# Five places for split output weights in the last pair, splits three ahead, mixed rows behind them

## The chip, the cores and the metric

The kernel runs on one NeuronCore of one Trainium2 chip. The metric is the device time of one execution in microseconds (us). PE is the matmul engine (TensorE), DVE is VectorE, ACT is ScalarE, POOL is GpSimd, and SP (SyncE) issues most of the DMAs. Each engine works through its own queue in order and is held to the others by semaphores alone, which are all written by hand in this kernel.

## The reference

One layer of a hybrid decoder trunk over 1024 tokens of width 2048, in fp32:

```
h = rms_norm(x, norm_g)
aq, ak, av, az, bq, bk, bv, bz, bf, cq, ck, cv, cz, cr = split(h @ w_in)
out_a = dilated_mixture(rms(aq), rms(ak), av)          # 12 heads, three dilated windows mixed
out_b = forgetting_attention(rms(bq), rms(bk), bv, cumsum(log_sigmoid(bf + bias)))   # 8 heads
out_c = rms(gla_chunked(cq, ck, cv, log_a))            # 4 heads, gated linear attention
mixed = concat(out_a * silu(az), out_b * silu(bz), out_c * silu(cz))
out   = x + mixed @ w_out
```

## The kernel before

**Split numbers.** Each fp32 product is made of three matmuls in a rounded format: an operand is split into a high part (ACT copies it into fp32r) and a low part (DVE subtracts), and PE does hi*hi, hi*lo and lo*hi. So a tile of weights must be loaded (SP), split by ACT, split by DVE, and then PE can use it. Such a weight tile is 128 x 512.

**Stages.** First x is normalised and transposed into `act_hi` and `act_lo` (16 rows k of 128 x 1024 each). Then projection groups run one after another: each has 16 k-steps in four quarters, and other work is woven between the quarters in eight slots a group. The work woven in is first that of the four GLA heads, then of ten attention pairs (two heads each; six of A, four of B). The last pair (`LAST` = 9) has only one projection group left (`S_LAST_Z`, slots 0 to 7). From slot 8 to 32 the output projection of the first 512 columns is woven in instead: 45 quarters called "early 0" to "early 44" here (`early_quarter`), in three rounds of 15. A round covers three, three and two token tiles (`ROUNDS`), since three PSUM banks are free, and goes through 15 of the 16 rows of the mixed activations. A quarter n of a round takes row k = `OUT_ORDER[n % 15]`. After the last pair come the first column group's remaining row (k=9), and the other column groups over all eight tiles (`out_quarter`).

**The mixed rows.** In slots 4 to 13 of the last pair the gated outputs of the heads are read back from DRAM over `act_lo`'s rows (`load_mixed`, two rows at a time) and split in place: ACT writes `act_hi`'s row, DVE `act_lo`'s (`mix_hi_part`, `mix_lo_part`, in the slot that `MIX_SLOT` gives). Row k=8 is that of the pair before and is taken from the tile `vz`. z of the last pair is loaded into `vz` only when this has been done, and its gate follows in slots 15 to 18.

**Places.** Raw output weights have four places (`EARLY_RAWS`), split ones three (`EARLY_SPLITS`): `w_hi`/`w_lo` have two, `extra_hi`/`extra_lo` one. ACT and DVE do the split of n+2 in the slot of early n. Their order inside a slot is: the pair's own steps with the mixed rows at their end, a split, the late steps of the slot, and the other splits.

**The pair's own steps** are written out by `steps_of`. An item j is one block of 128 queries of a head: scores on PE (L2038, L2040 for the causal part, L2041), bias and maximum on DVE (L1661), exponential on ACT (L1226), scaling on DVE (L1669, L1671). A unit u gathers such blocks: PE turns them (L2049), ACT and DVE split the result (L1234, L1677), and PE multiplies with the values (L2064). The steps that the prediction speaks of, by slot (a bar marks the late half; the early quarters stand where they are issued):

```
slot  8: product 1, scale 4, score 5, finish 1, early 0 | early 1
slot  9: scale 5, early 2 | early 3
slot 10: turn 2, early 4 | early 5
slot 11: product 2, turn 3, early 6 | score 6, early 7
slot 12: early 8 | product 3, scale 6, score 7
slot 13: early 9 | scale 7, early 10
slot 14: early 11 | turn 4, early 12
slot 15: early 13 | product 4, turn 5, early 14
slot 16: score 8, score 9, gate of the last pair, early 15 | early 16
slot 17: product 5, scale 8, scale 9, early 17
slot 18: turn 6, early 18 | early 19
slot 28: early 36 | scale 15, early 37
slot 29: early 38 | turn 10, early 39
```

**Early lines.** The early matmuls are L2113 to L2115, their splits L972 (ACT) and L1776 (DVE); a mixed row is L1334 (ACT) and L1797 (DVE); raw weights are loaded by L671, z by L471, the residual tiles by L716; sums of partials are L1791. The first column group's own splits are L958 and L1783, its matmuls L2154 to L2156.

**In a GLA head**, level l takes differences on DVE (L1519, L1520), exponentials on ACT (L1109), products on POOL (L881, L883) and eight matmuls on PE (L1945). DVE's masked copies into `weights_t` (L1568) follow each level; `put_first` does four of them for level 0 in one slot.

Of the kernel before, what the change touches and what calls it, by code (L numbers as in the profile page):

```python
# [15 lines left out]
P = 128  # L16
# [3 lines left out]
NT = SEQ // P  # L20
# [88 lines left out]

ROUNDS = ((0, 1, 2), (3, 4, 5), (6, 7))  # L110
EARLY = len(ROUNDS) * (KT - 1)
EARLY_RAWS, EARLY_SPLITS = 4, 3
EARLY_SLOT = [8 + (n * 5) // 9 for n in range(EARLY)]
MIX_SLOT = [4, 4, 5, 6, 6, 7, 8, 9, 9, 10, 10, 11, 12, 12, 13]

OUT_ORDER = list(range(LAST - 1)) + [LAST + 1, LAST + 2, LAST - 1] + list(range(LAST + 3, KT)) + [LAST]
KK_GATED = OUT_ORDER.index(LAST - 1)
MIX_LOADS = [k for k in range(0, KT, 2) if k != LAST - 1]
MIX_BUFS = 4
# [57 lines left out]
def score_offset(j):  # L177

    i = j % NT
    return HALF * (i % 2) if i < 4 else 0  # L180


def head_columns(c):
# [44 lines left out]
def build(nc, x, norm_g, w_in, a_q_gain, a_k_gain, b_q_gain, b_k_gain, fox_bias,  # L228
# [11 lines left out]
    with ExitStack() as ctx:  # L240
# [135 lines left out]
        last.close()  # L376

        early_raws = [extra_raw[:, 0, :], w_raw[:, 0, :], extra_raw[:, 1, :], w_raw[:, 1, :]]
        early_his = [w_hi[:, 0, :], extra_hi[:], w_hi[:, 1, :]]
        early_los = [w_lo[:, 0, :], extra_lo[:], w_lo[:, 1, :]]  # L380

        def mix_row(k):

# [76 lines left out]
        def _(sp):  # L460
# [278 lines left out]
            load_mixed(3)  # L739
            load_early_rows(2)  # L740
            load_early_rows(3)
            load_mixed(4)
            load_mixed(5)
            load_mixed(6)
            for n in range(4, EARLY):
                load_early_rows(n)
                if n == 6:
                    sp.wait_ge(mix_lo, KK_GATED + 1)
                    load_gate(LAST, last_column)
                if n == 7:  # L750

                    sp.wait_ge(silu_done, LAST)
                    for t in range(4):
                        load_early_residual(t)
                for r, tiles in enumerate(ROUNDS[:-1]):
                    if n == (KT - 1) * (r + 1) + 3:
                        for t in tiles:
                            store_partial(t)
                        for t in ROUNDS[r + 1]:
                            if t >= 4:  # L760
                                load_early_residual(t)
# [163 lines left out]
        def _(act):  # L925
# [20 lines left out]
            def split_hi_out(cg, kk):  # L946

                slot = kk % 2
                if kk == 1:

                    if isinstance(cg, int) and cg == 1:
                        act.wait_ge(partial_ready, NT)
                    else:
                        act.wait_ge(out_ready, NT * (cg - 1))
                else:
                    act.wait_ge(quarter_done, 3 * (GROUPS + AHEAD) + EARLY - len(ROUNDS) + (KT - 1) * (cg - 1) + kk - 1 + (kk == 0))
                act.wait_ge(w_in_sem[slot], 16 * (2 * (GROUPS + AHEAD) + EARLY // 4 + (KT // 2) * (cg - 1) + kk // 2 + 1))
                act.activation(w_hi[:, slot, :], w_raw[:, slot, :], ACT.Copy).then_inc(hi_done, 1)  # L958
# [332 lines left out]
            def last_body():  # L1291
                def steps(slot):
                    steps_at(LAST, 2 * slot, False)
                    for kk in range(KT - 1):
                        if MIX_SLOT[kk] == slot:
                            mix_hi_part(kk)

                def late(slot):
                    steps_at(LAST, 2 * slot + 1, False)

                def split_last(s, kq):
                    if kq < 4:
                        split_hi(s, kq)
                    else:
                        split_hi_early(0)

                group(S_LAST_Z, COL_B + 3 * B_WIDTH + (B_PAIRS - 1) * P, steps, split_after=split_last,
                      late=late)
                split_hi_early(1)
                for slot in range(8, SLOTS + 1):  # L1310
                    steps(slot)
                    for n in early_at(slot)[:1]:
                        split_next(n + 2)
                    late(slot)
                    for n in early_at(slot)[1:]:
                        split_next(n + 2)

            def split_next(n):
                if n < EARLY:
                    split_hi_early(n)  # L1320
                elif n == EARLY:
                    split_hi_out(1, 0)

            def mix_hi_part(kk):
                k = OUT_ORDER[kk]
                if k == LAST - 1:
                    act.wait_ge(o_done, LAST)
                    act.wait_ge(quarter_done, 3 * (S_LAST_Z + AHEAD) + k // 4 + 1)
                elif k == LAST:
                    act.wait_ge(o_done, LAST + 3)  # L1330
                else:
                    i = MIX_LOADS.index(k // 2 * 2)
                    act.wait_ge(mix_in[i % MIX_BUFS], 16 * (i // MIX_BUFS + 1))
                act.activation(act_hi[:, k, :], mix_row(k), ACT.Copy).then_inc(mix_hi, 1)  # L1334
# [20 lines left out]
        def _(dve):  # L1355
# [134 lines left out]
            def gla_steps(c, slot):  # L1490
# [19 lines left out]
                for l in range(LEVELS):  # L1510
                    if slot == G_LEVEL[l]:
# [6 lines left out]
                        dve.wait_ge(gla_ql, n - 1 if l >= 2 else LEVELS * c)  # L1518
                        dve.tensor_tensor(ev[:, :, 1, :], bv[:, :, 1, :], edge, ALU.subtract).then_inc(gla_diff, 1)  # L1519
                        dve.tensor_tensor(ev[:, :, 0, :], edge, bv[:, :, 0, :], ALU.subtract).then_inc(gla_diff, 1)  # L1520
                if slot == G_LEVEL[0] + 2:
                    put_first(c)
                for l in range(1, LEVELS - 1):
                    if slot == G_LEVEL[l] + 2:
                        put_level(c, l)
# [41 lines left out]
                dve.reg_add(levels_put, levels_put, 1)  # L1567
                dve.copy_predicated(dst, mask.bitcast(I32), data).then_inc(gla_put, 1)  # L1568

            def put_first(c):  # L1570
                dve.wait_ge(gla_zero, c + 1)
                dve.wait_ge(gla_lv, LEVELS * c + 1)
                for half in range(2):
                    to = weights_t[:, half * HALF:(half + 1) * HALF].rearrange("p (b u q) -> p b u q", b=2, u=2)
                    if half > 0:
                        dve.wait_ge(gla_put, levels_put)
                    put(to, ident_both[:, :, :].unsqueeze(1).broadcast_to([P, 2, 2, P]), pieces[half][:, :, :, 0:P])
                    dve.wait_ge(gla_put, levels_put)
                    put(to.rearrange("p b u (n two) -> p b u n two", two=2)[:, :, :, :, 1],
                        level_mask[:, 0, :, :].unsqueeze(1).broadcast_to([P, 2, 2, HEAD]),  # L1580
                        pieces[half][:, :, :, P:])

            def put_level(c, l):
                b = 1 << l
# [153 lines left out]
            def last_body():  # L1738
                def steps(slot):
                    steps_at(LAST, 1, 2 * slot, None)  # L1740
                    for kk in range(KT - 1):
# [12 lines left out]
                group(S_LAST_Z, steps, split_after=split_last, late=late)  # L1754
                split_lo_early(1)
                for slot in range(8, SLOTS + 1):
                    for n in early_at(slot):
                        if n % (KT - 1) == 0 and n > 0:
                            early_sums(n // (KT - 1) - 1)
                    steps(slot)  # L1760
                    for n in early_at(slot)[:1]:
                        split_next(n + 2)
                    late(slot)
                    for n in early_at(slot)[1:]:
                        split_next(n + 2)

            def split_next(n):
                if n < EARLY:
# [62 lines left out]
        def _(pe):  # L1831
# [191 lines left out]
            def score(pair, j, kind):  # L2023
                h, i = j // NT, j % NT
                n = (i + 1) * P
                if i == 0:
                    pe.wait_ge(ql_done, 2 * pair + h + 1)
                    pe.wait_ge(kl_done, 2 * pair + h + 1)
                    pe.wait_ge(k_other_done, 2 * pair + h + 1)

                if first_pair(pair) and i == 0:
                    pe.wait_ge(k_zeroed, h + 1)
                o = score_offset(j)
                pe.wait_ge(masked, ITEMS * pair + j - (o > 0))
                q = q_st[:, h, i * P:(i + 1) * P]
                for c0 in range(0, n, HALF):
                    c1 = min(c0 + HALF, n)
                    pe.matmul(scores[:, o + c0:o + c1], q, k_hi[:, h, c0:c1], start=True, stop=False)  # L2038
                    if kind == 1 and c1 == n:
                        pe.matmul(scores[:, o + i * P:o + n], ident_r[:], causal_r[:], start=False, stop=False)  # L2040
                    mm = pe.matmul(scores[:, o + c0:o + c1], q, k_lo[:, h, c0:c1], start=False, stop=True)  # L2041
                mm.then_inc(s_done, 1)
# [148 lines left out]
```

## Time and profile before

| | |
|---|---|
| median of 3 runs | 2104.77 us (2103.35 to 2106.62) |
| the profiled execution | 2104.9 us, span 2103.2 us |
| mean granted PE clock | 0.993 |
| busy PE / DVE / ACT / POOL | 2050.0 / 970.3 / 858.4 / 249.5 us |
| last pair from early 0 to the first column group | 1699.4 to 1831.7 us of the span |

Times in the trace are from the start of the span. A row of the timeline gives start, duration, engine, line, operation, tiles and shape, and in brackets how long the engine sat idle before it and what ended that. Matmuls are pipelined: the time that one takes is the distance to the start of the next, and its duration is modelled.

### The profile page before, as it was taken

To read this page: it belongs to the slowest core of one execution; us is meant where nothing else is said; L and a number is where in the kernel's file an instruction comes from. 1 tells how busy PE (TensorE), PEld (TensorE's weight loads), DVE (VectorE), ACT (ScalarE), POOL (GpSimd) and SP (SyncE) were. 2 spreads that over 40 slices of the span, in tenths; PEclk is the share of its full clock that TensorE was granted. 3 is DMA by queue.
4 is the path that set the end of the run, shared out by engine and by line. 5 is a ranking of instruction groups with operands and counts; after the bars stand their busy time and mean duration, and the time that the engine had idled before them with its cause. 6 is when DMAs were issued, how large, how long until landed. Compare 5 with 4: busy or idle time off the path is not lost.

```text
span 2103.2 us, 28249 instructions
## 1 busy us (share of the span) xinstructions
PE 2050.0 (97%) x10120; PEld 1717.1 (82%) x10120; DVE 970.3 (46%) x1579; ACT 858.4 (41%) x1434; POOL 249.5 (12%) x181
## 2 busy tenths in 40 slices
PE   6999999999999999999999999999999988999999
PEld 5778888888878888888888888888888867788887
DVE  6611356455544544554454544554544465512122
ACT  6311344434444444454544444454544454311110
POOL 0000344252420101010010101010010100000000
PEclk9999999999999999999999999999999999999999
DMA  6322323433232222222222222223222363324134
GB/s 224 78 75 65 108 76 104 108 89 108 69 101 76 71 88 58 86 74 89 61 70 85 75 86 86 81 81 100 60 90 85 129 210 113 125 89 130 47 128 150
DMA packets 192457, 201.09 MB, mean 96 GB/s; under 512 B 15993, under 2 KB 141993, under 8 KB 191233
## 3 DMA queue, kind: packets, MB, share of 16 engines
q1 hardware_dynamic: 175664, 169.70, 27.2%
q10 hardware_dynamic: 16720, 30.45, 3.9%
q8 instruction: 43, 0.70, 0.1%
q14 instruction: 30, 0.24, 0.0%
HBM read 151.33 MB, written 48.78 MB: 95 GB/s over the span
## 4 chain that ended last, share of the span: by engine, by line
PE 84%; DVE 7%; ACT 4%; issue 3%; DMA 2%; POOL 1%; SPq 0%; DVEq 0%; ACTq 0%; POOLq 0%
PE acc L1851 18%; PE acc L1853 18%; PE acc L1852 18%; PE pv L2064 4%; PE turned L2049 4%; PE scores L2041 2%; PE scores L2038 2%; DVE w_lo L1360 1%; PE scores L2154 1%; PE scores L2155 1%; PE turned L2155 1%; PE acc L2155 1%; PE scores L2156 1%; PE turned L2156 1%; PE acc L2156 1%
## 5 line engine op out<-in xcount | busy, mean ns | idle before, releaser
L1851 PE MATMUL acc<-act_hi,w_hi 128*128 128x512 f32 x1856 | 743.0, 400 | 7.5 <-DVE act_lo L1391 2.4
L1853 PE MATMUL acc<-act_hi,w_lo 128*128 128x512 f32 x1856 | 725.8, 391 | 0.0
L1852 PE MATMUL acc<-act_lo,w_hi 128*128 128x512 f32 x1856 | 724.2, 390 | 0.0
L1851 PEld LDWEIGHTS acc<-act_hi,w_hi 128*128 128x128 f32 x1856 | 349.4, 188 | 77.1 <-DVE w_lo L1360 5.0
L1853 PEld LDWEIGHTS acc<-act_hi,w_lo 128*128 128x128 f32 x1856 | 348.6, 188 | 76.1
L1852 PEld LDWEIGHTS acc<-act_lo,w_hi 128*128 128x128 f32 x1856 | 349.7, 188 | 65.1
L1360 DVE TENSOR_TENSOR w_lo<-w_raw,w_hi 128x512 fp32r<-128x512 f32 x223 | 196.2, 880 | 317.4 <-ACT w_hi L934 317.4
L1677 DVE TENSOR_TENSOR pt_lo<-turned,pt_hi 128x1024 fp32r<-128x1024 f32 (+1 forms) x120 | 114.9, 958 | 256.0 <-ACT pt_hi L1234 255.0
L1226 ACT ACTIVATE prob<-prob,neg_max 128x128 f32<-128x128 f32 (+7 forms) x160 | 124.1, 776 | 251.5 <-DVE neg_max L1661 251.5
L1234 ACT ACTIVATE pt_hi<-turned 128x1024 fp32r<-128x1024 f32 (+1 forms) x120 | 97.6, 813 | 244.7 <-PE turned L2049 244.7
L934 ACT ACTIVATE w_hi<-w_raw 128x512 fp32r<-128x512 f32 x223 | 139.0, 623 | 128.8 <-PE acc L1853 105.4
L908 POOL TENSOR_TENSOR q_st<-raw,q_st 64x1024 fp32r<-64x1024 f32 x20 | 49.4, 2472 | 994.1 <-ACT q_st L1203 994.1
L1661 DVE CUSTOM_DVE_ANT_0 prob<-scores,logit_bias 128x128 f32<-128x128 f32 (+7 forms) x160 | 118.2, 753 | 40.1 <-PE scores L2041 38.4
L1783 DVE TENSOR_TENSOR w_lo<-w_raw,w_hi 128x512 fp32r<-128x512 f32 x49 | 33.9, 693 | 213.9 <-ACT w_hi L958 213.9
L958 ACT ACTIVATE w_hi<-w_raw 128x512 fp32r<-128x512 f32 x49 | 31.0, 632 | 229.6 <-PE side L2156 209.8
L978 ACT ACTIVATE stage<-acc 128x512 f32<-128x512 f32 x112 | 66.7, 595 | 112.8 <-PE acc L1853 112.8
L2049 PE MATMUL turned<-ident,prob 128*128 128x128 f32 x720 | 100.2, 276 | 0.4 <-DVE prob L1671 0.3
L2049 PEld LDWEIGHTS turned<-ident,prob 128*128 128x128 f32 x720 | 85.2, 142 | 13.2 <-DVE prob L1671 2.4
L2064 PE MATMUL pv<-pt_lo,v_st 128*128 128x256 f32 (+1 forms) x400 | 94.2, 290 | 0.0
L2064 PE MATMUL pv<-pt_hi,v_st 128*128 128x256 f32 (+1 forms) x400 | 87.6, 269 | 0.3 <-DVE pt_lo L1677 0.3
L2038 PE MATMUL scores<-k_hi,q_st 128*128 128x512 f32 (+1 forms) x240 | 82.8, 347 | 3.9 <-DVE neg_max L1661 2.7
L1671 DVE TENSOR_SCALAR prob<-prob,inv_denom 128x128 f32<-128x128 f32 (+7 forms) x160 | 83.3, 521 | 5.7
(308 smaller groups left out, 2723.2 us busy)
## 6 DMA issues: line engine op xcount, KB each, us to landing
w_raw<-in_w_in_dram SPq DMA_DIRECT2D x240, 256.0 KB, 2.8
proj_scratch<-stage ACTq DMA_DIRECT2D x116, 256.0 KB, 2.1
w_raw<-in_w_out_dram SPq DMA_DIRECT2D x71, 256.0 KB, 3.0
raw<-proj_scratch SPq DMA_DIRECT2D x20, 512.0 KB, 3.2
act_lo<-mixed_scratch SPq DMA_DIRECT2D x7, 1024.0 KB, 6.7
res<-in_x_dram SPq DMA_DIRECT2D x24, 256.0 KB, 5.5
out_dram<-res SPq DMA_DIRECT2D x24, 256.0 KB, 2.8
extra_raw<-in_w_out_dram SPq DMA_DIRECT2D x23, 256.0 KB, 3.2
```

Source lines behind the costliest of these rows:

```text
L934: act.activation(w_hi[:, slot, :], w_raw[:, slot, :], ACT.Copy).then_inc(hi_done, 1)
L1226: act.activation(prob[:, j % 2, 0:n], prob[:, j % 2, 0:n], ACT.Exp, scale=-1.0, bias=neg_max[:, j:j + 1], accum_out=denom[:, j:j + 1]).the ...
L1234: act.activation(pt_hi[:, 0:n], turned[:, 0:n], ACT.Copy).then_inc(pth_done, 1)
L1360: dve.tensor_tensor(w_lo[:, slot, :], w_raw[:, slot, :], w_hi[:, slot, :].bitcast(F32), ALU.subtract)\
L1661: dve.tensor_tensor_reduce(out=prob[:, j % 2, 0:n], in0=scores[:, c0:c0 + n], in1=bias, scale=1.0, scalar=3e38, op0=ALU.add, op1=ALU.min, ...
L1677: dve.tensor_tensor(pt_lo[:, 0:n], turned[:, 0:n], pt_hi[:, 0:n].bitcast(F32), ALU.subtract)\
L1851: pe.matmul(acc, hi, xh, start=first, stop=False)
L1852: pe.matmul(acc, hi, xl, start=False, stop=False)
L1853: mm = pe.matmul(acc, lo, xh, start=False, stop=end)
L2038: pe.matmul(scores[:, o + c0:o + c1], q, k_hi[:, h, c0:c1], start=True, stop=False)
L2049: mm = pe.transpose(turned[:, o:o + P], prob[:, q, c * P:(c + 1) * P], ident[:])
L2064: mm = pe.matmul(pv[:, (2 * (d % 2) + q) * P:(2 * (d % 2) + 2) * P], v_st[:, h, c, :], (pt_hi, pt_lo)[part][:, o:o + (2 - q) * P], start=( ...
```

## The change

Four edits are made together.

1. **Output weights in the last pair.** Split weights have five places. The two new ones are halves of row k=9 (`LAST`) of `act_hi` and `act_lo`, which is not read from the last projection quarter that needs it until its own mixed row is written. ACT and DVE do the split of n+3 in the slot of early n. Mixed rows from slot 8 on are split at the end of their slot, behind the splits; the last three stand in slots 13, 14 and 14 and not in 12, 12 and 13. Row k=8 now comes ninth in the order of rows (it was the eleventh). SP loads the later mixed rows between the loads of raw weights, z of the last pair and four residual tiles behind raw weight 10 (before: behind 6 and 7), and stores partials two loads later.
2. **Waits that follow from it.** The first two splits of the first column group wait for the last quarter that used their place, and the mixed row of k=9 waits for all eight partials.
3. **Scores of item 4** (and 12) of every pair stand at column offset 128 of their two banks and not at 0, so that their 640 columns are done as 384 and 256 and not as 512 and 128.
4. **GLA**: the four masked copies of `put_first` are done in two slots, two in each.

```diff
-EARLY_RAWS, EARLY_SPLITS = 4, 3
+EARLY_RAWS, EARLY_SPLITS, EARLY_AHEAD = 4, 5, 3
-MIX_SLOT = [4, 4, 5, 6, 6, 7, 8, 9, 9, 10, 10, 11, 12, 12, 13]
-OUT_ORDER = list(range(LAST - 1)) + [LAST + 1, LAST + 2, LAST - 1] + list(range(LAST + 3, KT)) + [LAST]
+MIX_SLOT = [4, 4, 5, 6, 6, 7, 8, 9, 9, 10, 10, 11, 13, 14, 14]
+OUT_ORDER = list(range(LAST)) + list(range(LAST + 1, KT)) + [LAST]
...
-    return HALF * (i % 2) if i < 4 else 0
+    return HALF * (i % 2) if i < 4 else P * (i == 4)
...
-        early_his = [w_hi[:, 0, :], extra_hi[:], w_hi[:, 1, :]]
-        early_los = [w_lo[:, 0, :], extra_lo[:], w_lo[:, 1, :]]
+        early_his, early_los = ([w[:, 0, :], more, w[:, 1, :], row[:, LAST, 0:HALF], row[:, LAST, HALF:]]
+                                for w, more, row in ((w_hi, extra_hi[:], act_hi), (w_lo, extra_lo[:], act_lo)))
...
-            load_mixed(4)
-            load_mixed(5)
-            load_mixed(6)
             for n in range(4, EARLY):
+                if n < 7:
+                    load_mixed(n)
                 load_early_rows(n)
-                if n == 6:
+                if n == 10:
                     sp.wait_ge(mix_lo, KK_GATED + 1)
                     load_gate(LAST, last_column)
-                if n == 7:
+                if n == 10:
                     sp.wait_ge(silu_done, LAST)
                     for t in range(4):
                         load_early_residual(t)
                 for r, tiles in enumerate(ROUNDS[:-1]):
-                    if n == (KT - 1) * (r + 1) + 3:
+                    if n == (KT - 1) * (r + 1) + 5:
...
-                if kk == 1:
-                    if isinstance(cg, int) and cg == 1:
-                        act.wait_ge(partial_ready, NT)
-                    else:
-                        act.wait_ge(out_ready, NT * (cg - 1))
+                if isinstance(cg, int) and cg == 1 and kk < 2:
+                    user = (EARLY - 1 - 2 * kk) // EARLY_SPLITS * EARLY_SPLITS + 2 * kk
+                    act.wait_ge(quarter_done, 3 * (GROUPS + AHEAD) + user + 2 - len(ROUNDS))
+                elif kk == 1:
+                    act.wait_ge(out_ready, NT * (cg - 1))
...
-                split_hi_early(1)
+                for n in range(1, EARLY_AHEAD):
+                    split_hi_early(n)
                 for slot in range(8, SLOTS + 1):
                     steps(slot)
                     for n in early_at(slot)[:1]:
-                        split_next(n + 2)
+                        split_next(n + EARLY_AHEAD)
                     late(slot)
                     for n in early_at(slot)[1:]:
-                        split_next(n + 2)
+                        split_next(n + EARLY_AHEAD)
+                    mixed_of(slot)
...
                 elif k == LAST:
+                    act.wait_ge(partial_ready, NT)
                     act.wait_ge(o_done, LAST + 3)
...
-                if slot == G_LEVEL[0] + 2:
-                    put_first(c)
+                for half in range(2):
+                    if slot == G_LEVEL[0] + 2 + half:
+                        put_first(c, half)
...
-                for c0 in range(0, n, HALF):
-                    c1 = min(c0 + HALF, n)
+                edge = min(HALF - o % HALF, n)
+                for c0, c1 in ((0, edge), (edge, n))[:1 + (edge < n)]:
```

`last_body` is changed in the same way on DVE, with `mix_lo_part` and `split_lo_early`.

## Rows read from the trace of the kernel before

**Rows 1.** The page: busy time, share of the span and instructions of each engine.
```profile
PE 2050.0 (97%) x10120; PEld 1717.1 (82%) x10120; DVE 970.3 (46%) x1579; ACT 858.4 (41%) x1434; POOL 249.5 (12%) x181
```

**Rows 2.** Table by stretches: PE, PEld, DVE, ACT, POOL busy; granted clock; DMA.
```profile
1699.40:1755.90 56.50, 45.30 (x192) 36.03 (x193) 31.95 (x45) 24.75 (x36) 0.00 (x0) 0.88 0.39 133
...
1699.40:1831.70 132.30, 115.18 (x533) 93.27 (x533) 75.56 (x125) 57.40 (x94) 0.00 (x0) 0.94 0.40 132
```

**Rows 3.** PE's waits, 1690 to 1840: us in total, times, longest us.
```profile
PE acc L2113 <- DVE w_lo L1776: 11.5, 6, 3.7
PE acc L2113 <- DVE extra_lo L1776: 3.8, 2, 3.6
...
PE scores L2154 <- DVE w_lo L1783: 0.7, 1, 0.7
```

**Rows 4.** Timeline, ACT and PE before early 2: start, us, what, [idle before].
```profile
1704.07 1.04 ACT L1334 ACTIVATE act_hi<-act_lo 128x1024 fp32r<-128x1024 f32 x1
1705.02 0.62 ACT L972 ACTIVATE w_hi<-extra_raw 128x512 fp32r<-128x512 f32 x1
...
1707.03 0.79 PE L2113 MATMUL acc<-w_hi,act_hi 128*128 128x512 f32 x1 [3.23 <-DVE w_lo L1776]
```

**Rows 5.** Timeline, SP, ACT and PE around the weights of early 7.
```profile
1718.90 0.43 SPq L671 DMA_DIRECT2D w_raw<-in_w_out_dram  x1
...
1724.61 0.63 ACT L972 ACTIVATE extra_hi<-w_raw 128x512 fp32r<-128x512 f32 x1 [7.22 <-DMA w_raw<-in_w_out_dram]
...
1726.02 0.50 PE L2113 MATMUL acc<-extra_hi,act_hi 128*128 128x512 f32 x1 [3.60 <-DVE extra_lo L1776]
```

**Rows 6.** Timeline, PE: item 8's score; start of early 21; the turn after early 24.
```profile
1755.86 0.22 PE L2038 MATMUL scores<-k_hi,q_st 128*128 128x128 f32 x1
...
1774.32 0.39 PE L2113 MATMUL acc<-w_hi,act_hi 128*128 128x512 f32 x1
...
1782.59 0.93 PE L2049 MATMUL turned<-ident,prob 128*128 128x128 f32 x7
```

**Rows 7.** Timeline: DVE at unit 2's turn; ACT and PE before early 11.
```profile
1715.01 1.23 DVE L1677 TENSOR_TENSOR pt_lo<-turned,pt_hi 128x1024 fp32r<-128x1024 f32 x1 [2.72 <-ACT pt_hi L1234]
...
1740.20 0.61 ACT L972 ACTIVATE w_hi<-w_raw 128x512 fp32r<-128x512 f32 x1
...
1742.21 0.79 PE L2113 MATMUL acc<-w_hi,act_hi 128*128 128x512 f32 x1 [3.67 <-DVE w_lo L1776]
```

**Rows 8.** Timeline, PE and DVE around early 17 and unit 6's turn.
```profile
1764.13 0.50 PE L2113 MATMUL acc<-w_hi,act_hi 128*128 128x512 f32 x1 [1.39 <-DVE w_lo L1776]
...
1765.18 0.35 DVE L1671 TENSOR_SCALAR prob<-prob,inv_denom 128x256 f32<-128x256 f32 x1
...
1766.31 0.49 PE L2049 MATMUL turned<-ident,prob 128*128 128x128 f32 x3
```

**Rows 9.** Timeline, PE and DVE at early 38, and the 4 us after (columns of Rows 2).
```profile
1815.56 0.50 PE L2113 MATMUL acc<-w_hi,act_hi 128*128 128x512 f32 x1 [1.80 <-DVE w_lo L1776]
...
1815.62 0.75 DVE L1671 TENSOR_SCALAR prob<-prob,inv_denom 128x1024 f32<-128x1024 f32 x1
...
1816.00:1820.00 4.00, 4.00 (x16) 3.38 (x15) 1.57 (x3) 0.22 (x1) 0.00 (x0) 0.57 0.53 187
```

**Rows 10.** Timeline, PE: item 4's score in a pair, and the matmuls behind it.
```profile
685.46 0.39 PE L2038 MATMUL scores<-k_hi,q_st 128*128 128x512 f32 x1
...
686.09 0.45 PE L1851 MATMUL acc<-act_hi,w_hi 128*128 128x512 f32 x1
686.38 0.39 PE L1852 MATMUL acc<-act_lo,w_hi 128*128 128x512 f32 x1
```

**Rows 11.** GLA: mask copies (ns min/median/max); PE at level 3; PE's waits, 255 to 596.
```profile
L1568 DVE COPY_PREDICATED logit_bias<-ident_both,turned x4: 737/741/745, 261.4 to 521.5; 128x512 f32<-128x512 int32 x4
...
356.63 1.15 PE L1945 MATMUL side<-q_tile,k_level 96*128 96x128 f32 x8 [0.42 <-POOL q_tile L883]
...
PE side L1945 <- POOL q_tile L883: 2.0, 4, 0.7
```

More of the change, by code:

```diff
@@ L1293, in steps, with mixed_of @@
                     steps_at(LAST, 2 * slot, False)
+                    if slot < 8:
+                        mixed_of(slot)
+                def mixed_of(slot):
                     for kk in range(KT - 1):
@@ L1312, in last_body @@
                     for n in early_at(slot)[:1]:
-                        split_next(n + 2)
+                        split_next(n + EARLY_AHEAD)
                     late(slot)
                     for n in early_at(slot)[1:]:
-                        split_next(n + 2)
+                        split_next(n + EARLY_AHEAD)
+                    mixed_of(slot)
             def split_next(n):
@@ L1568, in put, with put_first @@
                 dve.copy_predicated(dst, mask.bitcast(I32), data).then_inc(gla_put, 1)
[L1570 to L1577, printed above, removed]
+            def put_first(c, half):
+                if half == 0:
+                    dve.wait_ge(gla_zero, c + 1)
+                    dve.wait_ge(gla_lv, LEVELS * c + 1)
+                to = weights_t[:, half * HALF:(half + 1) * HALF].rearrange("p (b u q) -> p b u q", b=2, u=2)
+                if half > 0:
                     dve.wait_ge(gla_put, levels_put)
-                    put(to.rearrange("p b u (n two) -> p b u n two", two=2)[:, :, :, :, 1],
-                        level_mask[:, 0, :, :].unsqueeze(1).broadcast_to([P, 2, 2, HEAD]),
-                        pieces[half][:, :, :, P:])
+                put(to, ident_both[:, :, :].unsqueeze(1).broadcast_to([P, 2, 2, P]), pieces[half][:, :, :, 0:P])
+                dve.wait_ge(gla_put, levels_put)
+                put(to.rearrange("p b u (n two) -> p b u n two", two=2)[:, :, :, :, 1],
+                    level_mask[:, 0, :, :].unsqueeze(1).broadcast_to([P, 2, 2, HEAD]), pieces[half][:, :, :, P:])
             def put_level(c, l):
@@ L1740, in steps, with mixed_of @@
                     steps_at(LAST, 1, 2 * slot, None)
+                    if slot < 8:
+                        mixed_of(slot)
+                def mixed_of(slot):
                     for kk in range(KT - 1):
@@ L1754, in last_body @@
                 group(S_LAST_Z, steps, split_after=split_last, late=late)
-                split_lo_early(1)
+                for n in range(1, EARLY_AHEAD):
+                    split_lo_early(n)
                 for slot in range(8, SLOTS + 1):
@@ L1761, in last_body @@
                     for n in early_at(slot)[:1]:
-                        split_next(n + 2)
+                        split_next(n + EARLY_AHEAD)
                     late(slot)
                     for n in early_at(slot)[1:]:
-                        split_next(n + 2)
+                        split_next(n + EARLY_AHEAD)
+                    mixed_of(slot)
             def split_next(n):
@@ L2033, in score @@
                 o = score_offset(j)
-                pe.wait_ge(masked, ITEMS * pair + j - (o > 0))
+                pe.wait_ge(masked, ITEMS * pair + j - (o == HALF))
                 q = q_st[:, h, i * P:(i + 1) * P]
-                for c0 in range(0, n, HALF):
-                    c1 = min(c0 + HALF, n)
+                edge = min(HALF - o % HALF, n)
+                for c0, c1 in ((0, edge), (edge, n))[:1 + (edge < n)]:
                     pe.matmul(scores[:, o + c0:o + c1], q, k_hi[:, h, c0:c1], start=True, stop=False)
```

## Prediction

> **What bounds the kernel now.** I read the page's busy times first: PE is busy 2050.0 of 2103.2 us, 97% [rows 1]. So only its idle time, its low clock and the work put on it can be changed, and I looked for these by stretches. The last pair's stretch (1699.4 to 1831.7) holds 17.1 us of the 53 idle ones, 11.2 of them in its first 56.5 us, where the mean granted clock is 0.88 [rows 2]. The table of waits shows that nearly all of it ends with L1776, the low part of a split of output weights: 11.5 us in six waits (3.23, 0.49, 3.67, 1.39, 0.95 and 1.80) and 3.8 in two [rows 3]. Below, "early n" is the n-th of the 45 steps of output projection woven into the last pair, and "split n" its two-part weight.
>
> The chip's clock first, as these rows show it: after the wait of 1.80 us, 4 us had a granted clock of 0.57, a mix of 1.2 and 2.4 GHz, which costs 4 x 0.43 = 1.7 us [rows 9]. After waits of 3.23 and 3.67 us the first matmul is modelled at 0.79 us, after 1.39 at 0.50 [rows 4, 7, 8]: the clock had fallen in the former and not in the latter. I price one such drop at 1.7.
>
> **The first round, early 0 to 14.** What is PE's own work there? Four quarters of three tiles (early 21 to 24) took 1782.59 - 1774.32 = 8.27 us, so one takes 2.07 [rows 6]. Fifteen are 31.0. Four turns, three products and two scores lie between them; from their columns, at the pace of these quarters (512 columns in 0.23 us) and a little more for the short ones, I estimate 2.6, 2.4 and 2.0. Together 38.0 us. The stretch from early 0 (1699.4) to item 8's score (1755.86) lasts 56.4 [rows 2, 6]. The loss is 18.4 us, waits and low clock.
>
> Three waits make most of it, each of another kind.
> - Early 2, 3.23 us: ACT's split 2 (1705.02) stands in its queue behind item 5's exponential and mixed row 6 (1704.07) [rows 4]. Split three ahead, split 2 is done before slot 8, and row 6 goes behind the splits. The wait goes.
> - Early 7, 3.60 us: SP waits for row k=8 to be mixed, loads z for the last pair, and the raw weights behind it were only issued at 1718.90, then shared the queue with four residual tiles; ACT waited 7.22 us for them, to 1724.61 [rows 5]. The edit puts z and residuals behind load 10, and row 8 is mixed two steps sooner. Load 11 is then the one behind them. By the walk below its split is wanted 7 us after its issue, against the 5.7 us that load 7 took. It is hidden; if it took 3 us longer, four further splits still wait ahead of PE.
> - Early 11, 3.67 us: item 7's exponential and a mixed row stand before split 11 (1740.20) [rows 7]. It goes the same way.
>
> What is late next? I walk the three queues with these durations: ACT 0.52 a split, 0.95 a mixed row; DVE 0.60 and 1.14; a full turn 0.93 and 1.15. Moving split 2 ahead delays item 5's scores by 0.6; split 3 gets ready 0.5 us after PE has done early 2. DVE then does row 6 before item 5's scaling, so unit 2's turn waits 0.65. Early 4 to 12 find weights and rows ready. Then comes the new one. In the new table rows 13 and 14 stand in slot 14, behind unit 4's turn and split 15. From the end of that turn ACT needs 1.0, DVE 1.15 for pt_lo, 0.6 for the split and 1.14 for row 13 (pt_lo's 1.23 is in [rows 7]; the next instruction starts 1.15 after it), with hand-overs about 4.1 us; PE has only early 12, 2.07. **Early 13 waits 2.05 us**, and after 1.80 the clock fell, so I add one drop of 1.7. New loss: 0.5 + 0.65 + 2.05 + 1.7 = 4.9. Gain of the round: 18.4 - 4.9 = 13.5.
>
> **The second and third round.** Early 15 waits for the partial sums whatever the split does: gain 0.2. The wait of early 17, 1.39, came from three gate activations before its split [rows 8]. Its split is now earlier, but two splits and two low parts still stand between the gate and item 9's scaling, which ended at 1765.18 + 0.35 = 1765.53. Unit 6's turn needs that, and started at 1766.31: no more than 0.78 can be won, and PE waits some 0.8 before the turn. Gain 0.7. Early 29's wait of 0.95 goes whole [rows 3]. Early 38's wait of 1.80 moves likewise: item 15's scaling ends at 1816.37, and unit 10's turn needs it. PE will have done early 38, 1.4 us, in the time it waited, and has about 1.45 us left to wait at the turn. That is nearest to 1.39, which caused no drop. Before, at full clock, early 38 would have ended at 1815.56 + 1.4 = 1816.96 [rows 9]: so 0.4 of waiting and the 1.7 of low clock are won, 2.1. The wait of 0.70 before the first full column group goes [rows 3], since its split and its load are issued two steps sooner. Sum: 0.2 + 0.7 + 0.95 + 2.1 + 0.7 = 4.6.
>
> **Places, rows, stores.** The two new places are in act_hi's row k=9, which nobody reads after the last projection; that row is mixed after the whole early part anyway, so the added wait on the 8 finished partials is met. Their cost is nothing. Stores of partials move two loads later; load 21 is behind them and wanted some 5 us after. Nothing.
>
> **Item 4's scores, in all ten pairs.** 640 columns from offset 0 made 512 and 128; from offset 128 they make 384 and 256. The old form takes 685.46 to 686.38 with the next projection matmul, 0.92 us, and that one alone is 0.29 instead of 0.23: a matmul of 128 columns is too short to cover the weight load behind it [rows 10]. By columns, two of 384 take 0.35, two of 256 some 0.24 to 0.29, the next 0.23: 0.82 to 0.87. Twenty items by 0.05 to 0.10: 1.0 to 2.0, I take 1.6. The Trainium skill (TensorE: Matmul & The Clock Gate, section Back-to-back issue gap) gives a stream cost by columns plus a fixed small part per matmul; by it both forms cost the same and this gain is nil. The row of 0.29 speaks for the trace's own price.
>
> **The first masks of a GLA head.** Four copies of 0.74 us stand before the difference for level 3, which feeds ACT, then POOL's q_tile, for which PE waits 0.42 in this head [rows 11]. Two of the copies, 1.5 us, go behind it; that is more than 0.42, and DVE's sum over the two slots is unchanged. All four such waits are 2.0 us [rows 11]. If POOL is the bound instead, the gain is nil; POOL had idled before the level, so I take 2.0.
>
> **Sum.** 13.5 + 4.6 + 1.6 + 2.0 = 21.7 us. The profiled execution took 2104.9 (the runs' median is 2104.77), so the forecast is **2083.2, say 2083 us**.
>
> **Rivals.**
> - *The walk holds* (60%): 2083. Without a drop of clock at early 13 it is 2081.5; without the small waits (0.5, 0.65, 0.8, 1.45) too, 2078; with a drop also at unit 10's turn 2085; with nothing from scores or masks 2087.
> - *The splits get in each other's way* (28%). ACT and DVE do the same work as before in less time (DVE is busy 31.95 us, which would be 78% of 41 us instead of 57%) [rows 2]; each waits for the other. If my walk misses three more hand-over waits of 1.8 with their drops, 3 x 3.5 = 10.5 comes back: 2094; one gives 2086.7. For it: each wait in these rows is such a chain. Against: three splits lie ready.
> - *It does little* (8%). If only the loads' order counted, only early 7's 3.60 and its drop 1.7 go, with 2.0 at the heads: 2097.6. Against: the splits named in [rows 4, 7] are plainly late by queue order.
> - *Slower* (4%). Every quarter from 6 to 14 needs a mixed row that now stands behind two splits. If DVE falls so far behind that each of the nine waits as early 13 does, each costs 2.05 + 1.7: 33.8 in all, the stretch lasts 38.0 + 1.15 + 33.8 = 73 us and not 56.4, +16.5, less the 8.2 of the rest: 2113. It decides from seven such quarters on. Against: by the walk rows 7 to 12 are ready 0.1 to 8 us before use.
>
> **Range and chances.** The likeliest case spans 2078 to 2087. With the second rival's nearer part the range is 2078 to 2094; above it lie the rest of that rival, "little" and "slower", together about 15%. Faster by over 0.2% (4.2 us; less than that a measurement of this kernel can't tell from no change): 0.93. Within: 0.03. Slower: 0.04.
>
> **What the profile after would show.** No wait on L1776 over 1 us between early 0 and 12. Load 7 issued right after split 3, z's load after load 10, no ACT wait on raw weights over 2 us. A wait of about 2 us before early 13 that ends with L1797, and a low clock behind it. Waits before turns (L2049) that end with L1671: 0.65, 0.8, 1.45 us. The stretch from early 0 to item 8's score near 43 us, from there to the first column group near 71 (75.8 before). The pairs before it about 1.4 us shorter, q_tile waits gone. Wrong would make it: a load 11 that lands after its split is due, DVE falling behind on mixed rows, or drops of clock after waits of about 1 us.

## The result, and the profile after

The change made the kernel very slightly slower: 2106.19 us against 2103.79 (medians of 22 runs each, of both kernels one after the other; one run of 4877.82 us stands apart from all others and is left out of the ratio), ratio 1.0015 with a 95% interval of 1.0009 to 1.0021. Forecast were 2083 us, range 2078 to 2094. The profiled execution of the changed kernel took 2107.99 us, its span is 2106.2, granted clock 0.991.

Lines have moved: a GLA head's differences are now L1524 and L1525 (before L1519, L1520), its products on POOL L880 and L882, its matmuls L1956, its mask copies L1574; the transposes of its state are L1968. In the last pair the early matmuls are L2124 to L2126, their splits L970 and L1787, a mixed row L1339 and L1808, a turn L2060, its product L2075.

The page's line of busy times, to be held against [rows 1]:

```profile
PE 2051.8 (97%) x10120; PEld 1721.6 (82%) x10120; DVE 977.9 (46%) x1579; ACT 859.4 (41%) x1434; POOL 242.3 (12%) x181
```

That says nearly nothing, so the span was cut at points that both kernels have. Tables by stretches (columns as in [rows 2]), the kernel before: all four GLA heads, and the first nine pairs.

```profile
250.00:596.00 346.00, 342.86 (x1749) 290.45 (x1747) 190.40 (x234) 155.69 (x260) 129.43 (x94) 1.00 0.35 95
609.58:1699.40 1089.82, 1085.38 (x5584) 918.25 (x5585) 545.99 (x1014) 521.36 (x882) 98.91 (x38) 1.00 0.27 85
```

The changed kernel: the heads, the nine pairs, early 0 to item 8's score, early 0 to the first column group (the last two answer to [rows 2]).

```profile
250.00:618.00 368.00, 355.05 (x1749) 301.09 (x1748) 198.09 (x233) 157.06 (x260) 122.29 (x94) 0.96 0.34 90
631.70:1719.70 1088.00, 1083.51 (x5584) 917.85 (x5584) 546.05 (x1014) 521.41 (x882) 98.94 (x38) 1.00 0.28 84
...
1719.70:1763.80 44.10, 39.36 (x191) 31.98 (x192) 32.34 (x46) 25.17 (x37) 0.00 (x0) 1.00 0.55 186
1719.70:1834.60 114.90, 106.44 (x531) 87.80 (x532) 75.49 (x125) 57.06 (x94) 0.00 (x0) 1.00 0.47 156
```

- From the start to the first pair's first score: 609.58 before, 631.70 after, **22.1 us longer**, all of it in the heads.
- The nine pairs: 1.8 us shorter.
- The last pair, from early 0 to the first column group: 132.3 to 114.9, 17.4 shorter by these edges (17.1 by the matmuls' own starts, 1831.67 and 1834.87).

So the planned gain is there, near its forecast of 18.1, and a loss somewhere else eats it. The sum, 22.1 - 1.8 - 17.1 = 3.2, agrees with the spans (3.0).

In the heads the same 1749 matmuls are done, but PE is idle 368.0 - 355.1 = 12.9 us and not 3.1, and busy 12.2 us longer for them at a mean clock of 0.96. PE's waits over the whole span (us in total, times, longest us); these three all lie in the heads, and the first answers to the 2.0 us of [rows 11]:

```profile
PE pv L1956 <- POOL q_tile L882: 6.4, 4, 1.9
...
PE scores L1968 <- ACT state L1110: 4.3, 3, 1.4
...
PE scores L1968 <- issue: 1.3, 1, 1.3
```

Now the place. Timeline of the kernel before, DVE and POOL, in the slots of the first masks (second head):

```profile
347.37 1.42 POOL L881 TENSOR_TENSOR k_level<-g_k,g_t 96x256 f32<-96x256 f32 x2
348.14 0.74 DVE L1568 COPY_PREDICATED logit_bias<-ident_both,turned 128x512 f32<-128x512 int32 x1
348.75 1.28 POOL L883 TENSOR_TENSOR q_tile<-g_qd,g_t 96x512 f32<-96x512 f32 x1
349.00 0.73 DVE L1568 COPY_PREDICATED logit_bias<-level_mask,turned 128x256 f32<-128x256 int32 x1
...
350.51 0.68 DVE L1519 TENSOR_TENSOR g_t<-g_b 96x512 f32<-96x512 f32 x1
351.11 0.68 DVE L1520 TENSOR_TENSOR g_t<-g_b 96x512 f32<-96x512 f32 x1
...
352.82 0.72 DVE L1519 TENSOR_TENSOR g_t<-g_b 96x512 f32<-96x512 f32 x1
352.95 2.31 POOL L881 TENSOR_TENSOR k_level<-g_k,g_t 96x256 f32<-96x256 f32 x2 [2.92 <-ACT g_t L1109]
353.46 1.22 DVE L1520 TENSOR_TENSOR g_t<-g_b 96x512 f32<-96x512 f32 x1
```

The same of the changed kernel, with ACT's and PE's rows in which it ends:

```profile
353.46 1.87 POOL L880 TENSOR_TENSOR k_level<-g_k,g_t 96x256 f32<-96x256 f32 x2
...
354.67 1.21 DVE L1524 TENSOR_TENSOR g_t<-g_b 96x512 f32<-96x512 f32 x1
355.30 1.72 POOL L882 TENSOR_TENSOR q_tile<-g_qd,g_t 96x512 f32<-96x512 f32 x1
355.81 1.76 DVE L1525 TENSOR_TENSOR g_t<-g_b 96x512 f32<-96x512 f32 x1
357.49 0.73 DVE L1574 COPY_PREDICATED logit_bias<-ident_both,turned 128x512 f32<-128x512 int32 x1
...
359.19 1.33 DVE L1574 COPY_PREDICATED logit_bias<-level_mask,side 128x512 f32<-128x512 int32 x1
...
360.31 1.62 DVE L1524 TENSOR_TENSOR g_t<-g_b 96x512 f32<-96x512 f32 x1
...
365.54 1.72 POOL L882 TENSOR_TENSOR q_tile<-g_qd,g_t 96x512 f32<-96x512 f32 x1
...
367.39 1.15 PE L1956 MATMUL pv<-q_tile,k_level 96*128 96x128 f32 x8 [1.49 <-POOL q_tile L882]
...
368.80 1.04 ACT L1110 ACTIVATE state<-g_v 96x1024 f32<-96x1024 f32 x1
...
369.98 0.58 PE L1968 MATMUL scores<-ident,g_v 96*128 96x96 f32 x2 [1.43 <-ACT state L1110]
```

And the clock behind the two waits, 4 us each (columns as in [rows 2]; the granted clock is the 0.67 and the 0.50):

```profile
368.00:372.00 4.00, 2.57 (x18) 2.38 (x18) 2.26 (x4) 3.73 (x5) 3.02 (x3) 0.67 0.00 0
372.00:376.00 4.00, 4.00 (x13) 3.30 (x13) 1.39 (x1) 2.60 (x5) 2.77 (x5) 0.50 0.00 0
```

What is to be seen:
1. Before, all four copies (from 346.42 on) ran while POOL was busy, the first beside the end of level 1, the others in the main beside level 2 (347.37 to 350.03). They read PSUM, and take 0.72 to 0.74 whether POOL works, as here, or stands still, as behind 357.49 in the changed kernel. When the level-3 differences came, POOL was idle: 0.68 each.
2. After, only two copies are ahead. The differences now fall on POOL's level-2 products and take 1.21 and 1.76: 1.61 us more.
3. The two copies that were moved (357.49 to 359.19, 1.70 us) now stand ahead of level 4's difference. It starts 360.31 - 354.67 = 5.64 after level 3's; before, 352.82 - 350.51 = 2.31. The 3.33 between them are those 1.61 and 1.70.
4. Level 3 itself is in time (PE's wait of 0.42 is gone). Level 4's q_tile is 1.49 late. Level 5's exponential is late too, ACT's copy of the state stands behind it, and the state's transposes wait another 1.43.
5. Then the clock falls: after idling 1.49 and, eight matmuls of 128 columns later, 1.43 us, PE has a granted clock of 0.67 and then 0.50 (1.2 GHz). An 18 us stretch around these waits shows 0.81 in every head: 0.19 x 18 = 3.4 us a head.

All four heads show it; the two waits are 1.91 and 1.31 in the first head, 1.48 or 1.49 and 1.43 in the others. Waits, 6.4 + 4.3 + 1.3 - 2.0 = 10.0, and low clock, 4 x 3.4 = 13.7, make 23.7 at most (a stretch's clock counts idle time too), against 22.1.

The chip's rule that stands behind point 2 is in the Trainium skill (SBUF — State Buffer, section Who interferes with whom): a DVE instruction with two inputs in SBUF contends with a GpSimd instruction that reads SBUF. The section calls the shared ports an exclusive lock. The rows agree, and to the hundredth each subtraction ends the same time behind the product that it met: k_level ends at 353.46 + 1.87 = 355.33 and the first difference at 354.67 + 1.21 = 355.88; q_tile ends at 357.02 and the second difference at 357.57. That is 0.55 both times. The copies, with one operand in PSUM, are not held.

### The profile page after: what moved, and what is told of

Read it like the earlier page. It is cut to its first block, busy times and chain, and to the rows that moved or that the text cites. A ratio compares the mean times of both kernels' runs of the same rounds, so it can differ in the third digit from the quotient of the medians.

```text
span 2106.2 us, 28248 instructions
## 1 busy us (share of the span) xinstructions
PE 2051.8 (97%) x10120; PEld 1721.6 (82%) x10120; DVE 977.9 (46%) x1579; ACT 859.4 (41%) x1434; POOL 242.3 (12%) x181
## 4 chain that ended last, share of the span: by engine, by line
PE 84%; DVE 7%; ACT 4%; issue 3%; DMA 2%; SPq 0%; POOL 0%; ACTq 0%; DVEq 0%; POOLq 0%
PE acc L1862 18%; PE acc L1864 18%; PE acc L1863 18%; PE pv L2075 4%; PE turned L2060 4%; PE scores L2052 2%; PE scores L2049 2%; DVE w_lo L1365 1%; PE scores L2165 1%; PE turned L2165 1%; PE acc L2165 1%; PE scores L2166 1%; PE acc L2166 1%; PE turned L2166 1%; PE turned L2167 1%
## 5 line engine op out<-in xcount | busy, mean ns | idle before, releaser
L2060 PE MATMUL turned<-ident,prob 128*128 128x128 f32 x720 | 98.6, 273 | 3.1 <-DVE prob L1676 3.0
L2060 PEld LDWEIGHTS turned<-ident,prob 128*128 128x128 f32 x720 | 83.4, 141 | 16.3 <-issue 5.5
L2075 PE MATMUL pv<-pt_lo,v_st 128*128 128x256 f32 (+1 forms) x400 | 94.3, 290 | 0.0
L2075 PE MATMUL pv<-pt_hi,v_st 128*128 128x256 f32 (+1 forms) x400 | 87.8, 269 | 2.6 <-DVE pt_lo L1682 2.6
L2049 PE MATMUL scores<-k_hi,q_st 128*128 128x128 f32 (+2 forms) x240 | 82.8, 348 | 3.9 <-DVE neg_max L1666 2.7
```

The lines of the kernel that those rows point to most:

```text
L2060: mm = pe.transpose(turned[:, o:o + P], prob[:, q, c * P:(c + 1) * P], ident[:])
L2075: mm = pe.matmul(pv[:, (2 * (d % 2) + q) * P:(2 * (d % 2) + 2) * P], v_st[:, h, c, :], (pt_hi, pt_lo)[part][:, o:o + (2 - q) * P], start=( ...
```

## The experiments

Each ran on the chip beside the kernel before; ratios are to that.

**The GLA masks: whole again in the changed kernel, and split alone in the kernel before.**

```diff
 e1_copies_whole: the changed kernel
-                for half in range(2):
-                    if slot == G_LEVEL[0] + 2 + half:
-                        put_first(c, half)
+                if slot == G_LEVEL[0] + 2:
+                    for half in range(2):
+                        put_first(c, half)
 e2_copies_alone: the kernel before
-                if slot == G_LEVEL[0] + 2:
-                    put_first(c)
+                for half in range(2):
+                    if slot == G_LEVEL[0] + 2 + half:
+                        put_first(c, half)
...
```

> The changed kernel with the four mask copies of a GLA head back in one slot; the last pair and item 4's scores stay changed. If the moved copies cost all that was lost (the heads' stretch grew from 86.9 to 92.0 us a head), each head returns to 86.9 and the time falls by about 21 us to 2085. If the longer heads come from something else in the change, or the last pair gives its gain back, it stays near 2106. If half of it is a chance effect, 2095.

> The kernel before with the two-slot mask copies as the only edit. If these alone lengthen each head by 5.3 us: 2104 + 21 = 2125. If they only cost together with another part of the change: 2104. By the prediction's own step (four waits of 2.0 us in all go): 2102.

Measured: e1 2085.18 us, ratio 0.9921 (0.9896 to 0.9946); e2 2122.16, ratio 1.0091 (1.0065 to 1.0117). The edit costs 2106.19 - 2085.18 = 21.0 us in the changed kernel and 2122.16 - 2103.96 = 18.2 in the kernel before (19.8 and 19.1 by the ratios). In e1 the waits for q_tile are 2.0 us in 4 again, and the heads have their old stretch:

```profile
250.00:596.00 346.00, 342.77 (x1747) 290.11 (x1747) 189.74 (x232) 155.72 (x261) 129.38 (x94) 1.00 0.35 95
```

e2's waits for q_tile are 6.2 us in 4 and for the state 4.3 in 3. The whole loss is this edit's, in either kernel.

**Contention or queue order?** Two kernels, both from the changed one. e3 keeps two slots, but puts the second pair of copies at the head of its slot, ahead of level 3's differences. e4 leaves DVE's order as the change made it and lets POOL begin level 2 only when DVE has done level 3's differences.

```diff
 e3_second_before_diff
+                if slot == G_LEVEL[0] + 3:
+                    put_first(c, 1)
                 for l in range(LEVELS):
                     if slot == G_LEVEL[l]:
...
-                for half in range(2):
-                    if slot == G_LEVEL[0] + 2 + half:
-                        put_first(c, half)
+                if slot == G_LEVEL[0] + 2:
+                    put_first(c, 0)
 e4_pool_waits
                     pool.wait_ge(gla_decay, n + 1)
+                    if l == 2:
+                        pool.wait_ge(gla_diff, 2 * (LEVELS * c + 3) + 2)
```

> The changed kernel, but the second two copies stand at the head of the next slot, before level 3's differences on DVE. Theory of shared access (DVE's differences run at half speed while POOL multiplies level 2): the copies, which read PSUM, cover POOL's work again, level 3's differences start when POOL is nearly done and take 0.68 us each again: heads of 87 to 88 us, 2085 to 2089. Theory that it is the split of the copies over two slots as such, the pause between them or the later free banks: 2106.

> The changed kernel, with one wait added: POOL starts level 2's products only when DVE has done level 3's differences. The order of DVE's work is that of the changed kernel. Theory of shared access: the differences take 0.68 us each and not 1.2 to 1.8, level 4 comes 1.6 us earlier, its wait of 1.5 us on PE and the one behind it vanish; POOL's level 2 is 1 to 2 us later, which its 1.4 us of slack nearly cover: 2085 to 2092. Theory of order alone (the two copies stand before level 4's difference, whatever its speed): level 4's wait stays, 2106 or more, since POOL now starts later too.

Measured: e3 2084.94, ratio 0.992 (0.9896 to 0.9945), the same as e1: two slots as such cost nothing. e4 2089.4, ratio 0.994 (0.9923 to 0.9958). Timelines of e4, DVE and PE:

```profile
349.91 0.68 DVE L1526 TENSOR_TENSOR g_t<-g_b 96x512 f32<-96x512 f32 x1
350.50 0.68 DVE L1527 TENSOR_TENSOR g_t<-g_b 96x512 f32<-96x512 f32 x1
...
358.67 1.22 DVE L1526 TENSOR_TENSOR g_t<-g_b 96x512 f32<-96x512 f32 x1
359.81 1.77 DVE L1527 TENSOR_TENSOR g_t<-g_b 96x512 f32<-96x512 f32 x1
```

```profile
363.76 0.38 PE L1970 MATMUL scores<-ident,g_v 96*128 96x96 f32 x2 [1.27 <-ACT state L1112]
```

With POOL made to start *later*, the kernel is 2106.19 - 2089.4 = 16.8 us faster (15.8 by the ratios): the two differences are back at 0.68, the wait for q_tile is gone in three heads (0.6 left in one), and the clock stays up (0.998 over the span). That settles contention as what pushed the chain over the edge. It isn't all: the moved copies are still ahead of level 4, and 3.8 us in three waits for the state remain, with 1.2 in the first head. Level 5's differences run beside POOL in e4 (1.22 and 1.77), but they did so in the kernel before too (1.21 and 1.22, at 356.97 and 358.11), so only 0.56 of that is new. The waits in the heads are 5.6 us (3.8 + 1.2 + 0.6) against e1's 2.0; these 3.6 are most of the 4.2 us between e4 and e1. So the copies' place in the queue costs 4 to 5 us at most (by the runs and by the spans, 2087.7 and 2082.7) when level 3's differences run free, and the rest of the loss comes only with contention there.

**Item 4's scores alone, and the last pair alone**, each on the kernel before.

```diff
 e5_scores_alone
-    return HALF * (i % 2) if i < 4 else 0
+    return HALF * (i % 2) if i < 4 else P * (i == 4)
...
-                for c0 in range(0, n, HALF):
-                    c1 = min(c0 + HALF, n)
+                edge = min(HALF - o % HALF, n)
+                for c0, c1 in ((0, edge), (edge, n))[:1 + (edge < n)]:
 e6_last_pair_alone: items 1 and 2 of the change, without items 3 and 4
```

> The kernel before with item 4's scores at offset 128 as the only edit. By the trace's price of a short matmul (weight load not covered) 0.05 to 0.10 us an item, 20 items: 1.0 to 2.0 us less, ratio 0.9991 to 0.9995; the pairs' stretch of the profile 1.4 us shorter. By a price in columns alone: no change.

> The kernel before with the last pair's edit alone (places, splits ahead, order of rows, loads). Theory: it gives what the changed kernel's own stretch shows, 1699.42 to 1831.67 before and 1719.73 to 1834.87 after, 17.1 us: 2087. Rival: part of it is only given since the heads come later in the changed kernel, and the gain is under 14: above 2090.

Measured: e5 2100.12 (12 runs) against 2102.61 (17), ratio 0.9987 (0.9979 to 0.9996). Timeline of PE in e5, to be held against [rows 10]:

```profile
685.74 0.33 PE L2038 MATMUL scores<-k_hi,q_st 128*128 128x384 f32 x1
...
686.32 0.39 PE L1851 MATMUL acc<-act_hi,w_hi 128*128 128x512 f32 x1
686.55 0.39 PE L1852 MATMUL acc<-act_lo,w_hi 128*128 128x512 f32 x1
```

The four score matmuls (two of 384 columns, two of 256) and the next one take 0.81 us and not 0.92; 20 x 0.11 = 2.2 us. e6: 2087.43, ratio 0.9926 (0.9913 to 0.9939), so 15.5 us (12.8 to 18.3) by the runs; by the profiled spans 2103.2 - 2085.7 = 17.5.

**What is still lost in the last pair.** The changed kernel's waits on PE there, to be held against [rows 3]:

```profile
PE turned L2060 <- DVE prob L1676: 3.0, 4, 1.5
PE pv L2075 <- DVE pt_lo L1682: 2.6, 2, 2.1
PE acc L2124 <- DVE act_lo L1808: 1.9, 2, 1.5
```

Its timeline (SP, ACT, then PE's rows at product 2, early 13 and unit 10's turn):

```profile
1721.72 0.39 SPq L709 DMA_DIRECT2D act_lo<-mixed_scratch  x1
1722.15 0.47 SPq L671 DMA_DIRECT2D extra_raw<-in_w_out_dram  x1
...
1731.21 0.63 ACT L970 ACTIVATE extra_hi<-extra_raw 128x512 fp32r<-128x512 f32 x1 [2.50 <-DMA extra_raw<-in_w_out_dram]
1731.75 1.05 ACT L1339 ACTIVATE act_hi<-act_lo 128x1024 fp32r<-128x1024 f32 x1
1732.69 1.04 ACT L1339 ACTIVATE act_hi<-vz 128x1024 fp32r<-128x1024 f32 x1
1733.76 1.03 ACT L1232 ACTIVATE pt_hi<-turned 128x1024 fp32r<-128x1024 f32 x1
...
1736.47 0.36 PE L2075 MATMUL pv<-pt_hi,v_st 128*128 128x256 f32 x1 [2.10 <-DVE pt_lo L1682]
...
1757.87 0.47 PE L2124 MATMUL acc<-act_hi 128*128 128x512 f32 x1 [1.52 <-DVE act_lo L1808]
...
1823.09 1.06 PE L2060 MATMUL turned<-ident,prob 128*128 128x128 f32 x8 [1.48 <-DVE prob L1676]
```

(0.5 us of the second line is a wait ahead of early 0.) The load of two mixed rows (1721.72) stands ahead of raw weight 6 (1722.15), whose split starts 9 us after its issue. ACT is held 2.50 us for it, and behind it in ACT's queue are two mixed rows and unit 2's pt_hi, so product 2 waits 2.10. Two small edits, the second on top of the first:

```diff
 e7_mixed_later: e1 with the last mixed load two weights later
-                if n < 7:
-                    load_mixed(n)
+                if n < 6 or n == 8:
+                    load_mixed(n if n < 6 else 6)
 e8_row13_earlier: e7 with
-MIX_SLOT = [4, 4, 5, 6, 6, 7, 8, 9, 9, 10, 10, 11, 13, 14, 14]
+MIX_SLOT = [4, 4, 5, 6, 6, 7, 8, 9, 9, 10, 10, 11, 13, 13, 14]
 e9_all: e8 with e3's place of the copies
```

> The run with the copies whole, and the last 1 MB pair of mixed rows loaded before raw weight 8 and not before raw weight 6. Theory: the wait of ACT for raw weight 6 (2.50 us in the changed kernel) comes from that megabyte just ahead of it, and it is what makes product 2 wait 1.8 us: both go, 2083.3. Rival: DVE's own queue (the two mixed rows before unit 2's turn) keeps product 2 waiting: 2085, or the load only moves its delay to raw weight 8.

> The run before it (mixed_later), with mixed row 13 in slot 13 and not in slot 14. Theory: early 13's wait of 1.5 us goes, since the row no longer stands behind unit 4's turn and split 15; row 12, split 14 and the turn's low part come up to 0.5 later: 1.0 to 1.5 us less than mixed_later, near 2082. Rival: what is won at early 13 is lost at early 12 or product 4: no difference.

> row13_earlier with the second two copies of a GLA head at the head of the next slot, before level 3's differences (where that run showed q_tile waits of 1.4 us in place of 2.0). If these add up it is the fastest kernel of the study, 0.3 to 0.6 us below row13_earlier, near 2081.5; the difference is small beside the scatter.

Measured: e7 2084.15, ratio 0.991 (0.9897 to 0.9923); e8 2082.23, ratio 0.9901 (0.9887 to 0.9916), span 2079.6; e9 2082.45, ratio 0.9905 (0.989 to 0.9921). By the runs, e7 can't be told from e1, nor e9 from e8. In the traces product 2's wait is gone in e7, and early 13's in e8; the largest that e8 has left in the last pair are the turns':

```profile
PE turned L2060 <- DVE prob L1676: 3.1, 4, 1.5
```

e8 is the fastest measured, 20.4 us under the kernel before (2102.61 beside it).

**Which part of the last pair's edit carries it?** Both from e1: splits only two ahead, and z with the residuals behind raw weights 6 and 7 as before.

```diff
 e10_two_ahead
-EARLY_RAWS, EARLY_SPLITS, EARLY_AHEAD = 4, 5, 3
+EARLY_RAWS, EARLY_SPLITS, EARLY_AHEAD = 4, 5, 2
 e11_z_early
-                if n == 10:
+                if n == 6:
                     sp.wait_ge(mix_lo, KK_GATED + 1)
...
-                if n == 10:
+                if n == 7:
                     sp.wait_ge(silu_done, LAST)
```

> The run with the copies whole, but splits only two ahead, five places kept. If the lookahead is what removed the waits of early 2, 11, 17, 29 and 38, most of them return (about 3 + 0.5 + 1 + 2 us and drops of clock), though the rows now stand behind the splits: 2089 to 2095. If the order of rows and loads did it, the time stays within 1 us of 2085.

> The run with the copies whole, but z of the last pair and the four residual tiles again behind raw weights 6 and 7. If the late z is needed for the gain, early 7's wait returns with part of its size (3.6 us before; row 8 is mixed two steps sooner now), with a drop of clock: 2087 to 2090. If three splits ahead cover it: 2085.

Measured: e10 2092.46, ratio 0.9949 (0.9935 to 0.9962); e11 2094.41, ratio 0.9957 (0.9944 to 0.9971). Against e1's 0.9921 they give back 5.9 and 7.6 us; e1's interval overlaps theirs at its end, but no run of e10 (2088.73 and up) or e11 (2093.22 and up) is as short as e1's longest, 2087.91. PE's waits in e10's last pair, then in e11's:

```profile
PE acc L2124 <- DVE act_lo L1787: 3.2, 2, 2.2
PE acc L2124 <- DVE w_lo L1787: 3.1, 2, 1.7
PE acc L2124 <- DVE act_lo L1808: 2.2, 1, 2.2
```

```profile
PE turned L2060 <- DVE prob L1676: 5.5, 5, 2.4
PE pv L2075 <- DVE pt_lo L1682: 2.8, 3, 1.6
```

Without the third split ahead PE waits for splits, as before. With z early ACT stands 6.26 and 3.33 us at late raw weights (to 1720.50 and 1724.46); two waits for splits come back, 1.49 and 1.60, as the expectation had it, and the waits for turns and products grow too, since the pair's own steps stand behind those splits in ACT's queue. Both parts are needed. The new order of rows and the later slots of the last mixed rows weren't tried alone.

## Why the prediction was wrong

**The step that failed** is "The first masks of a GLA head": "Two of the copies, 1.5 us, go behind it; that is more than 0.42, and DVE's sum over the two slots is unchanged", taken as a gain of 2.0 us. It is a loss of 22.1 in the trace (e1 and e2: 18 to 21 by the runs), 24.1 us from what was forecast. It failed in three places.
- DVE's sum is not unchanged. Durations were carried over from a time when POOL was idle to one when it was not. The trace before already had such a subtraction at 0.68 (350.51 and 351.11) and at 1.22 (353.46, beside POOL's level 3); I took it for granted that moving an instruction leaves its length alone.
- I looked at what the copies stood in front of (level 3) and not at what they were moved in front of (level 4's difference, and behind it level 5's and the state). Level 3's wait went, as forecast, and one 3.5 times as long came one level later.
- The bound "if POOL is the bound instead, the gain is nil" allowed no loss: in none of the rivals did the heads lose time, and the range left the measured time outside by 12 us.

**The first round of the last pair**: forecast about 43 us, measured 44.1 (56.5 before), so a gain of 12.4 and not 13.5. Right in mechanism. Early 2, 7 and 11 don't wait; early 3 waits 0.25 (0.5 forecast), unit 2's turn 0.41 (0.65), early 12 0.42 (0), early 13 1.52 (2.05). "No ACT wait on raw weights over 2 us" and "early 4 to 12 find weights and rows ready" were wrong for weight 6: the load of mixed rows ahead of it was left out of the walk, and product 2 waits 2.10. PE's own work there is 39.4 us (its busy time at a clock of 1.00) and not the estimated 38.0; the waits are 4.7 and not 3.2; the drop of clock priced behind early 13, 1.7, didn't come. Two errors are cancelled in part by the third: that the forecast is only about 1 us off is partly luck.

**The second and third round**: forecast 71 us, measured 114.9 - 44.1 = 70.8 (75.8 before). Unit 6's turn waits 0.85 (0.8 forecast), unit 10's turn 1.48 (1.45), early 15 0.73, where it was 0.72 before, so the 0.2 forecast for it didn't come; early 29's and 38's waits and the one before the column group are gone, 0.37 before early 30 is new, and unit 8's turn waits 0.29 (0.31 before).

**Places, rows, stores** at nothing: no wait in the trace speaks against it; it wasn't tried alone.

**Item 4's scores**: forecast 1.6 (1.0 to 2.0), measured 2.2 by e5's rows and 1.8 in nine pairs; the runs give 2.7, from 0.8 to 4.4. The mechanism holds. By the formula for one matmul's gap in the Trainium skill (TensorE: Matmul & The Clock Gate, section Back-to-back issue gap) both forms would cost the same; the measured 0.11 us an item decides against it here. The same section says that the formula counts too little for short matmuls, since the weight load isn't in it, which the prediction left out. The rows agree: the matmul behind 128 columns takes 0.29 us, the one behind 256 takes 0.23.

**The rivals** about the last pair: "the splits get in each other's way" foresaw three more waits with drops of clock; one came, without a drop. "Does little" and "slower" are refuted by e6. It gains 15.5 us (12.8 to 18.3) by the runs; the forecast's own terms for it, 13.5 + 4.6 = 18.1, are at the upper end. With the heads left alone (e1) the kernel lies at 2085.18, inside the range: it is the item of 2 us, and not those that made up most of the sum, that decided it.

## What to carry to other kernels

When an instruction is moved in a queue, look at what the *neighbouring* engine does at its new place: here a subtraction of DVE with both operands in SBUF was held to the end of POOL's product, and a masked copy out of PSUM wasn't, so such copies belong where POOL is busy. Follow the queue to the end of the dependent chain and not only to the wait that is to go, for what is taken from in front of one level stands in front of the next. And a small edit in a part where PE hardly waits deserves a bound on the side of loss as wide as any other: here an item forecast at 2 us decided the sign.

## What the runs showed of the hardware

- The same 96x512 subtraction on DVE takes 0.68 us with POOL idle and 1.21 to 1.77 beside POOL's products. POOL is lengthened too: its two k_level products take 1.42 us beside PSUM copies and 1.87 beside a weight's split and the first of these subtractions, its q_tile 1.28 and 1.72.
- Holding POOL back made the kernel 16.8 us faster (e4).
- A single wait of 2.10 us and one of 1.52 were followed by no drop of clock (granted 1.00 over the stretch), while one of 1.80 was [rows 9]. Two waits with 1.15 us of matmuls between them, 1.49 and 1.43 (1.91 and 1.31 in the first head), were followed by one in each of four heads. A wait's length alone doesn't foretell it.
- Two times 640 columns take 0.11 us less as 384 and 256 (0.81) than as 512 and 128 (0.92), with the matmul behind them counted in.
